# A two-part encoder layer on one core: attention, output projection and router input as one pipeline over token tiles

## The chip, the cores and the metric

One NeuronCore of a Trainium2 chip runs the whole layer as one program. It has five engines that work side by side, each on its own list of instructions, strictly in order: TensorE (PE, matmuls and transposes, results into eight PSUM banks of 128 x 512 f32), VectorE (DVE), ScalarE (ACT), GpSimd (POOL) and SyncE (SP, which only issues transfers). They are tied together by semaphores. The metric is the device time of one execution in microseconds (us), lower is better.

## The reference

```
h = rms_norm(x, g) * (1 + sc1) + sh1            # x: 512 tokens x 1024; sc, sh, g1, g2 = silu(c) @ w_ada + b_ada
proj = h @ w_in                                 # 1024 -> 1024 (gMLP u, v) + 672 (latents of attention)
gm_out = u * (tril(W_s) @ LN(v) + b)            # 512 channels
q, k, v = latents, normalised, @ w_q_up, w_kv_up   # 8 heads, 96 wide, v 64 wide; QK-norm and rotary
mla_out = softmax(q k^T, chunk-causal) v        # 512 channels; token tile t sees key tiles 0..t
mixed = concat(rms_norm(gm_out), rms_norm(mla_out))
x = x + g1 * (mixed @ w_out)                    # 1024 x 1024
h2 = rms_norm(x, g) * (1 + sc2) + sh2
scores = sigmoid(h2 @ w_router)                 # 64 experts, group-limited top 8
x = x + g2 * (shared_expert(h2) + sum over the 8 chosen experts of w_e * expert_e(h2))
```

Everything is f32. Where the kernel needs full precision at TensorE's faster rate it splits an operand into an upper part (rounded to the short format) and a lower part (the rest), and makes three matmuls of one: upper x upper, upper x lower, lower x upper (`three_passes`).

## The kernel before

The 512 tokens are T = 4 tiles of 128; D = 1024 is C = 8 chunks of 128. The program is written by hand for each engine, and the order of the work on an engine is the order in which its block is written; nothing is scheduled by a planner.

The stages, in time: (1) twelve 2 MB blocks of `w_ada` arrive; blocks 0 and 2 are multiplied on PE (L613), the ten others on DVE (`ada_block`, L1229 to L1234, eight multiply-adds each) and summed over partitions by one matmul with ones; after block 3 the first normalised input `h` can be formed. (2) The input projections with f32 weights (L633), the up-projections of q, k and v, QK-norm and rotary on DVE (L1303 to L1324), transposes of q and k. Meanwhile POOL makes the upper and lower parts of `w_out` (L509, L511), two chunks at a time. (3) Attention, 32 heads-of-tiles i = 0..31, tile t = i // 8 in the order 0, 1, 2, 3. For each: `scores` on PE (one f32 matmul of (t+1)*128 columns into one of NSB = 4 banks), `row_max` on DVE (a memset of the masked corner and a reduce), `exponential` on ACT, `prob_transposes` on PE, `prob_copy` on ACT, `weighted_values` on PE. PE runs three scores ahead. After the fourth head of the next tile DVE turns the finished tile into `mixed` (`outputs`, L1344 to L1349). (4) When all tiles are through, one root on ACT, one reciprocal on DVE, the scaling of `mixed`, 32 transposes of it in six banks (L744), its upper part on ACT (L1066) and its lower part on DVE (L1370), for all 512 tokens at once. (5) The output projection: 8 groups of 24 matmuls (L574 to L576), and behind each tile on DVE the residual and the second norm (`residual` L1382 to L1385, `norm2` L1389 to L1391, with a root on ACT between). (6) Transposes of `h2` (L768), router (L778), sigmoid, then the choice of experts on DVE (L1400 to L1434), while PE computes the shared expert (L787). (7) A list of the rows of each expert is made on DVE by 16 rounds of MAX8 (L1518 to L1523), and (8) the 64 experts run one after the other: 3 MB of weights each, split into upper parts on ACT (L1103, L1109) and lower parts on DVE (L1466), rows gathered and scattered by indirect transfers of POOL.

What the change touches is (1), the making of the parts of `w_out` in (2), and all of (3) to (6), with SP's list for the stores of `h2` and the loads behind them. The loop over the experts in (8) keeps its instructions.

Of the kernel before, what the change touches and what calls it, by code (L numbers as in the profile page):

```python
# [29 lines left out]
P = 128  # L30
# [16 lines left out]
def trunk_kernel(nc, a, out):  # L47
# [21 lines left out]
    ADA_PE = (0, 2)  # L69
    ADA_DVE = tuple(j for j in range(ADA) if j not in ADA_PE)  # L70
    ADA_FIRST = 4
    MAXX = 32
    NSMALL = 9
    scale = float(QD) ** -0.5
# [5 lines left out]
    with ExitStack() as ctx:  # L80
# [48 lines left out]
        NSB, NTB = 4, 2  # L129
# [8 lines left out]
        mixT_high = at("mixT_high", 80, [P, C, S], F32R)  # L138
        mixT_low = at("mixT_low", 159, [P, C, S], F32R)
        h2 = at("h2_sb", 143, [P, T, D])  # L140
        h2T = at("h2T", 112, [P, C, S])
# [7 lines left out]
        sco = at("sco", 151, [P, T, NE])  # L149
        bia = at("bia", 152, [P, T, NE])  # L150
        rep = at("rep", 153, [P, T, NE])
        m8 = at("m8", 154, [P, T * N_GROUPS, 8])
# [20 lines left out]
        w_d = [at(f"w_d{i}", 72 + 8 * i, [P, FC, D]) for i in range(2)]  # L173
        gu_high = [at(f"gu_high{half}", kb, [P, 2, HC, FF], F32R) for half, kb in enumerate((16, 88))]
        gu_low = [at(f"gu_low{half}", kb, [P, 2, HC, FF], F32R) for half, kb in enumerate((24, 102))]
        d_high = at("d_high", 112, [P, FC, D], F32R)
        d_low = at("d_low", 120, [P, FC, D], F32R)
# [24 lines left out]
        def small(name, shape, dt=F32):  # L202
# [13 lines left out]
        epsc = small("epsc", [P, 1])  # L216
        freq = small("freq", [P, RH])
# [53 lines left out]
        (s_mm, nmax_ok, exp_ok, pT_tr, pT_ok, av_mm, o_ok, mix_v, oss_ok, ostd_ok, orstd_ok, mix_ok, mixT_tr, out_mm,  # L271
         x1_ok, ss2_ok, std2_ok, h2_ok, st_h2, h2T_tr, h2T_ok, rt_mm, sco_ok, selm_ok, pos_mm, lmat_ok, list_mm,
         list_ok) = (sem(n) for n in (
            "s_mm", "nmax_ok", "exp_ok", "pT_tr", "pT_ok", "av_mm", "o_ok", "mix_v", "oss_ok", "ostd_ok", "orstd_ok", "mix_ok",
            "mixT_tr", "out_mm", "x1_ok", "ss2_ok", "std2_ok", "h2_ok", "st_h2", "h2T_tr", "h2T_ok", "rt_mm",
            "sco_ok", "selm_ok", "pos_mm", "lmat_ok", "list_mm", "list_ok"))
        flip_set, key_ok, key_tr, found_ok, found_tr, foundT_ok, flip_mm, src_ok, wts_ok, st_w, w_ok = (sem(n) for n in (
            "flip_set", "key_ok", "key_tr", "found_ok", "found_tr", "foundT_ok", "flip_mm", "src_ok", "wts_ok", "st_w", "w_ok"))
# [99 lines left out]
        def _(sp):  # L378
            sp.dma_start(cT[:], a["c"].rearrange("b (p c) -> p (b c)", c=C)).then_inc(ld["c"], 16)
            w_in_v = a["w_in"][0].rearrange("(p c) n -> p c n", c=C)  # L380
            for j in range(ADA):
                i, _ = ada_buffer(j)
                if j >= ADA_FIRST:
                    before = j - ADA_FIRST if j < ADA_FIRST + 2 else j - 2
                    if before in ADA_PE:
                        sp.wait_ge(ada_pe, ADA_PE.index(before) + 1)
                    else:
                        sp.wait_ge(ada_dve, ADA_DVE.index(before) + 1)
# [1247 lines left out]
```

## Time and profile before

| | us |
|---|---|
| three runs | 1123.85, 1121.76, 1113.04 |
| median | 1121.76 |
| the profiled execution, whole | 1113.93 |
| its span, first to last instruction | 1112.0 |
| PE, DVE, ACT, POOL busy in the span | 971.8, 905.2, 602.3, 278.4 |

The profile page gives busy time by engine, the span in 40 slices, the costliest groups of instructions, and the chain of waits that ended last. "PEclk" is the granted TensorE clock as a share of 2.4 GHz; it has two levels, 1.00 and 0.50. A busy PE is not a PE at its peak: a matmul's record runs to its modelled end and overlaps the next, so the pace is read from the starts. The whole time of an execution is 1.9 us more than its span here.

### The profile page before, as it was taken

The numbers are of one execution on the slowest core, as the hardware profiler recorded it, in microseconds if no ns is written. First come the engines' busy times: TensorE is split into PE (matmuls) and PEld (weight loads), VectorE is DVE, ScalarE is ACT, GpSimd is POOL, SyncE is SP. The second block draws the span as 40 slices with busy tenths as digits, with TensorE's granted clock in tenths as the row PEclk, the third lists the DMA queues.
The fourth block names the chain that finished last, engine by engine and source line by source line (L and its number), as shares of the span: only waits on it lengthen the run. The fifth ranks groups of instructions, "written<-read, shape, count | busy, mean of one in ns | idle before, by whom it ended". The sixth has DMA issues, their size and how long they took to land.

```text
span 1112.0 us, 14197 instructions
## 1 busy us (share of the span) xinstructions
PE 971.8 (87%) x4335; PEld 745.7 (67%) x4336; DVE 905.2 (81%) x1280; ACT 602.3 (54%) x948; POOL 278.4 (25%) x186
## 2 busy tenths in 40 slices
PE   3797899898999979898999988989897999898895
PEld 1354375586788657677777777777676777677684
DVE  3687877754566878998999999999998899898894
ACT  1123153466113046676777766667675767676672
POOL 1004105130000202323234232332323232324232
PEclk9899899889999989999999999999999999999897
DMA  9976402200027278999999999999999999999973
GB/s 310 393 280 232 151 1 76 104 2 1 19 89 276 67 294 268 374 318 339 325 340 359 344 333 339 326 337 333 327 349 327 309 333 356 351 327 350 341 257 59
DMA packets 86232, 286.79 MB, mean 258 GB/s; under 512 B 18052, under 2 KB 18564, under 8 KB 77112
## 3 DMA queue, kind: packets, MB, share of 16 engines
q1 hardware_dynamic: 64240, 248.03, 61.1%
q0 software_dynamic: 19056, 36.89, 13.2%
q10 hardware_dynamic: 2904, 1.48, 0.5%
q8 instruction: 16, 0.26, 0.1%
q14 instruction: 16, 0.13, 0.0%
HBM read 283.04 MB, written 37.88 MB: 289 GB/s over the span
## 4 chain that ended last, share of the span: by engine, by line
DMA 49%; PE 29%; DVE 11%; issue 6%; ACT 1%; SPq 1%; POOL 1%; POOLq 0%; DVEq 0%; ACTq 0%
DMA out<-oute,src_tab 44%; PE bank L633 5%; PE bank L574 4%; PE bank L575 4%; PE bank L576 4%; DMA xe<-h_rows,src_tab 3%; DMA ada_w<-in_w_ada 2%; DVE ada_acc L1234 2%; PE bank L787 2%; PE bank L708 2%; PE bank L725 1%; DVE gu_low L1466 1%; DVE q_sb L1313 1%; PE bank L804 1%; PE bank L716 1%
## 5 line engine op out<-in xcount | busy, mean ns | idle before, releaser
L1466 DVE TENSOR_TENSOR gu_low<-w_gu,gu_high 128x1024 fp32r<-128x1024 f32 x256 | 301.4, 1218 | 10.6 <-ACT gu_high L1103 5.4
L1103 ACT CAST gu_high<-w_gu 128x1024 fp32r<-128x1024 f32 x256 | 256.6, 1055 | 62.8 <-PE bank L576 57.2
L530 POOL DMA_INDIRECT out<-oute,src_tab x64 | 128.9, 2015 | 465.0 <-DMA out<-oute,src_tab 357.5
L574 PE MATMUL bank<-gu_high,xeT_high 128*128 128x512 f32 x512 | 208.1, 406 | 2.8 <-DVE xeT_low L1466 2.6
L576 PE MATMUL bank<-gu_high,xeT_low 128*128 128x512 f32 x512 | 202.1, 395 | 0.0
L575 PE MATMUL bank<-gu_low,xeT_high 128*128 128x512 f32 x512 | 201.8, 394 | 0.0
L1466 DVE TENSOR_TENSOR d_low<-w_d,d_high 128x1024 fp32r<-128x1024 f32 x128 | 150.4, 1216 | 0.0
L1109 ACT CAST d_high<-w_d 128x1024 fp32r<-128x1024 f32 x128 | 128.1, 1053 | 18.0 <-PE bank L576 18.0
L820 PE MATMUL bank<-ident,xe 128*128 128x128 f32 x512 | 73.5, 288 | 60.3 <-DMA xe<-h_rows,src_tab 58.4
L820 PEld LDWEIGHTS bank<-ident,xe 128*128 128x128 f32 x512 | 64.5, 194 | 81.3 <-issue 77.6
L574 PE MATMUL bank<-d_high,hwT_high 128*128 128x512 f32 x256 | 112.3, 439 | 6.7 <-DVE hwT_low L1466 6.5
L1466 DVE TENSOR_TENSOR xeT_low<-bank,xeT_high 128x512 fp32r<-128x512 f32 x128 | 82.2, 684 | 42.8 <-ACT xeT_high L1119 40.9
L574 PEld LDWEIGHTS bank<-gu_high,xeT_high 128*128 128x128 f32 x512 | 97.2, 190 | 23.1 <-DVE xeT_low L1466 2.7
L576 PEld LDWEIGHTS bank<-gu_high,xeT_low 128*128 128x128 f32 x512 | 96.7, 189 | 22.6
L575 PEld LDWEIGHTS bank<-gu_low,xeT_high 128*128 128x128 f32 x512 | 96.8, 189 | 19.9 <-issue 0.2
L524 POOL DMA_INDIRECT xe<-h_rows,src_tab x64 | 95.9, 1499 | 50.1 <-issue 45.7
L576 PE MATMUL bank<-d_high,hwT_low 128*128 128x512 f32 x256 | 106.7, 417 | 0.0
L575 PE MATMUL bank<-d_low,hwT_high 128*128 128x512 f32 x256 | 106.0, 414 | 0.0
L1119 ACT CAST xeT_high<-bank 128x512 fp32r<-128x512 f32 x128 | 68.9, 590 | 63.5 <-PE bank L820 63.5
L1502 DVE TENSOR_TENSOR oute<-bank,mod_rows 128x512 f32<-128x512 f32 x128 | 82.0, 682 | 10.8 <-PE bank L576 10.7
L1234 DVE SCALAR_TENSOR_TENSOR ada_acc<-ada_w,cact,ada_acc 128x512 f32<-128x512 f32 x70 | 64.2, 918 | 2.5
L574 PEld LDWEIGHTS bank<-d_high,hwT_high 128*128 128x128 f32 x256 | 52.5, 205 | 16.8 <-DVE d_low L1466 4.6
(278 smaller groups left out, 1291.6 us busy)
## 6 DMA issues: line engine op xcount, KB each, us to landing
w_gu<-in_w_exp_gate SPq DMA_DIRECT2D x128, 512.0 KB
w_gu<-in_w_exp_up SPq DMA_DIRECT2D x128, 512.0 KB
w_d<-in_w_exp_down SPq DMA_DIRECT2D x64, 1024.0 KB, 8.6
ada_w<-in_w_ada SPq DMA_DIRECT2D x12, 2048.0 KB, 11.9
w_out_sb<-in_w_out SPq DMA_DIRECT2D x2, 2048.0 KB, 7.2
w_lat_sb<-in_w_in SPq DMA_DIRECT2D x1, 2688.0 KB, 21.9
x_sb<-in_x SPq DMA_DIRECT2D x1, 2048.0 KB, 24.2
w_v_sb<-in_w_in SPq DMA_DIRECT2D x1, 2048.0 KB, 10.3
```

The costliest lines, as they stand in the source:

```text
L524: pool.indirect_dma_start(xe[i][:], None, h2_dram, bass.IndirectOffsetOnAxis(ap=rows, axis=0), bounds_check=last_row, oob_is_err=False).th ...
L530: pool.indirect_dma_start(out_rows, bass.IndirectOffsetOnAxis(ap=rows, axis=0), oute[i][:], None, bounds_check=last_row, oob_is_err=False, ...
L574: pe.matmul(dst, xh, wh, start=start, stop=False)
L575: pe.matmul(dst, xh, wl, start=False, stop=False)
L576: return pe.matmul(dst, xl, wh, start=False, stop=stop)
L820: last = pe.transpose(bank[c // 4][:, c % 4 * P:(c % 4 + 1) * P], xe[b][:, c:D:C], ident[:])
L1103: act.copy(gu_high[half][:, m], w_gu[half][i][:, m]).then_inc(gu_high_ok[half], 1)
L1109: act.copy(d_high[:, m], w_d[i][:, m]).then_inc(d_high_ok, 1)
L1119: act.copy(xeT_high[i][:, m * HC:(m + 1) * HC, :], bank[m][:].rearrange("p (c n) -> p c n", c=HC)).then_inc(xe_high_ok, 1)
L1234: ins = dve.scalar_tensor_tensor(acc[n % 2][:], w[:, c, :], cact[:, c:c + 1], acc[n % 2][:], ALU.mult, ALU.add)
L1466: return dve.tensor_tensor(low, whole, high.bitcast(F32), ALU.subtract)
L1502: last = dve.tensor_tensor(oute[i][:, cols], bank[4 + m][:], mod[:, GATE2, cols], ALU.mult)
```

## The change

The 32 heads are still 32, but the tiles go 3, 2, 1, 0 (`TILES`), the tile with most keys first; p is the place in that order. Scores use two banks instead of four (NSB = 2) and PE runs two scores ahead; one bank holds the weighted values, one (`T_BANK`) all transposes, two the output projection. While tile p is in attention, the finished tile p-1 goes through normalisation, transposes, split and output projection, and tile p-2 through residual, second norm, transposes and router. On each engine a function `between_heads(p, hd)` says what comes behind head hd of tile p. The roots of both norms no longer go to ACT: DVE computes them with a bit trick and three Newton steps (`rsqrt_mean`, 12 instructions on one or two columns). The gain `out_norm_g` moves from `mixed` into the weights: ACT forms the upper part of `w_out` times gain (8 x 128x1024), POOL scales the chunk and subtracts (8 + 8 instructions of 128x1024, where it had 4 + 4 of 128x2048). In (1) `x` is loaded first, each of blocks 0 to 3 is halved between PE and DVE, and the gain row is finished in two halves. PE's first half of the shared expert's first product stands ahead of the last router transposes; SP waits for the last score before it loads the shared weights and for the last output projection before it goes on to the experts' weights; the store of the last tile of `h2` moves to POOL.

```diff
-        NSB, NTB = 4, 2
+        NSB, NTB = 2, 2
+        O_BANK, T_BANK, Y_BANK = 4, 5, 6
+    TILES = tuple(reversed(range(T)))
+    W_ORDER = tuple(range(C // 2, C)) + tuple(range(C // 2))
 # SP
+            store_h2(0)
+            store_h2(1)
+            sp.wait_ge(s_mm, NI)
...
+            store_h2(2)
+            sp.wait_ge(out_mm, 2 * T)
 # POOL
+            for n in range(C):
+                c = W_ORDER[n]
                 pool.wait_ge(wout_high_ok, n + 1)
+                pool.tensor_scalar(w_out[:, c], w_out[:, c], on_g[:, c:c + 1], None, ALU.mult).then_inc(wout_scaled, 1)
+                pool.wait_ge(wout_scaled, n + 1)
+                pool.tensor_tensor(w_out_low[:, c], w_out[:, c], w_out_high[c // 2][:, c % 2].bitcast(F32), ALU.subtract).then_inc(wout_ok, 1)
 # PE
+            OUT_CUTS = (0, 3, 6, 9, 12, 2 * C)
+            def between_heads(p, hd):
+                if p >= 1:
+                    if hd in (1, 2):
+                        mixed_transposes(p - 1, hd - 1)
+                    if hd >= 3:
+                        out_projection(p - 1, OUT_CUTS[hd - 3], OUT_CUTS[hd - 2])
+                if p >= 2:
+                    if hd in (4, 5):
+                        h2_transposes(p - 2, hd - 4)
+                    if hd == 6:
+                        router(p - 2)
 # ACT
+            def between_heads(p, hd):
+                if p == 0 and hd < C // 2:
+                    wout_high(C // 2 + hd)
+                if p >= 1 and hd in (1, 2):
+                    mixed_high(p - 1, hd - 1)
+                if p >= 2:
+                    if hd in (4, 5):
+                        h2T_copy(p - 2, hd - 4)
+                    if hd == 6:
+                        logits(p - 2)
 # DVE
+            def rsqrt_mean(col, n):
+                k = col.shape[1]
+                y, sq, half = root[:, 0:k], root_sq[:, 0:k], root_half[:, 0:k]
+                link(dve.tensor_scalar(col, col, 1.0 / n, EPS, ALU.mult, ALU.add))
+                dve.tensor_scalar(half, col, -0.5, None, ALU.mult)
+                link(dve.tensor_scalar(y.bitcast(I32), col.bitcast(I32), -0.5, float(0x5F375A86), ALU.mult, ALU.add))
+                for step in range(3):
+                    link(dve.tensor_tensor(sq, y, y, ALU.mult))
+                    link(dve.tensor_tensor(sq, sq, half, ALU.mult))
+                    link(dve.scalar_tensor_tensor(y if step < 2 else col, sq, 1.5, y, ALU.add, ALU.mult))
+            def between_heads(p, hd):
+                if p >= 1:
+                    if hd == 0:
+                        outputs(p - 1)
+                    if hd in (1, 2):
+                        mixed_low(p - 1, hd - 1)
+                if p == 1 and hd == 3:
+                    second_gain()
+                if p >= 2:
+                    if hd == 2:
+                        residual(p - 2)
+                    if hd == 3:
+                        norm2(p - 2)
+                if hd == 6:
+                    link(square_sum(p, 0))
+            row_max(0)
+            for i in range(NI):
+                if i + 1 < NI:
+                    row_max(i + 1)
+                between_heads(*divmod(i, H))
```

DVE before, around the fourth head of a tile: a score's maximum is a MEMSET and a TENSOR_REDUCE, and `outputs` of the tile before stands between two of them once in eight heads.

```order
L1339 MEMSET bank 64x64 [waits s_mm]
L1340 TENSOR_REDUCE nmax<-bank 128x1 [waits dve_step]
L1344 RECIPROCAL den<-den 128x8 [waits av_mm]
L1345 TENSOR_TENSOR mixed<-bank,den 128x512 [waits dve_step]
L1349 ISA osq,oss<-mixed 128x512 [waits o_ok]
L1349 ISA oss 128x1
L1349 ISA osq,oss<-mixed 128x512
L1349 ISA oss 128x1
L1339 MEMSET bank 64x64 [waits s_mm,dve_step]
L1340 TENSOR_REDUCE nmax<-bank 128x1 [waits dve_step]
```

DVE now, behind `outputs` (which has grown by `rsqrt_mean` and two scalings), heads 0 to 3 of tile place p = 2.

```order
L1435 TENSOR_SCALAR mixed<-mixed,oss 128x512
L1406 MEMSET bank 64x64 [waits s_mm]
L1407 TENSOR_REDUCE nmax<-bank 128x1 [waits dve_step]
L1440 TENSOR_TENSOR mixT_low<-bank,mixT_high 128x512 [waits mixT_high_ok]
L1406 MEMSET bank 64x64 [waits s_mm]
L1407 TENSOR_REDUCE nmax<-bank 128x1 [waits dve_step]
L1440 TENSOR_TENSOR mixT_low<-bank,mixT_high 128x512 [waits mixT_high_ok]
L1449 TENSOR_TENSOR xtmp<-bank,mod_rows 128x512 [waits out_mm]
L1451 TENSOR_TENSOR x_sb<-x_sb,xtmp 128x512 [waits x1_ok]
L1449 TENSOR_TENSOR xtmp<-bank,mod_rows 128x512 [waits out_mm,dve_step]
L1451 TENSOR_TENSOR x_sb<-x_sb,xtmp 128x512 [waits x1_ok]
L1406 MEMSET bank 64x64 [waits s_mm,dve_step]
```

So the maximum of each of the next three scores now stands behind a step that itself waits for ACT, or behind four or more full-width operations.

PE now, heads 1 and 2 of the second tile in the order: the transposes of `mixed` stand between a head's weighted values and the next score.

```order
L707 MATMUL bank<-kT,qT 128x384 [waits exp_ok]
L715 MATMUL bank<-ident,prob_91 128x128 [waits pT_ok,exp_ok]
L715 MATMUL bank<-ident,prob_91 128x128 x2
L725 MATMUL bank<-vv_sb,probT_93 128x64 [waits pT_ok]
L725 MATMUL bank<-vv_sb,probT_93 128x64 x2
L738 MATMUL bank<-ident,mixed 128x128 [waits mix_ok]
L738 MATMUL bank<-ident,mixed 128x128 x3
L707 MATMUL bank<-kT,qT 128x384 [waits exp_ok]
L715 MATMUL bank<-ident,prob_92 128x128 [waits pT_ok,exp_ok]
L715 MATMUL bank<-ident,prob_92 128x128 x2
```

Before, nothing but scores, transposes and weighted values stood on PE between the first score and the last head.

## Rows read from the trace of the kernel before

**Rows 1.** Windows by stage: stretch, length, busy time of each engine, granted clock, DMA share, GB/s.
```profile
219.00:271.00 52.00, 51.14 (x304) 42.08 (x304) 25.63 (x82) 34.20 (x99) 12.37 (x4) 0.86 0.00 1
271.00:285.00 14.00, 6.17 (x35) 5.88 (x34) 10.15 (x20) 8.30 (x14) 0.00 (x0) 0.76 0.00 0
285.00:328.50 43.50, 43.50 (x193) 35.97 (x193) 21.93 (x30) 0.88 (x3) 0.00 (x0) 1.00 0.09 37
328.50:340.00 11.50, 11.17 (x99) 10.99 (x98) 5.29 (x7) 5.92 (x11) 0.00 (x0) 1.00 0.87 323
340.00:354.00 14.00, 14.00 (x69) 12.32 (x68) 9.92 (x61) 6.17 (x8) 2.05 (x4) 1.00 0.99 379
436.00:1112.00 676.00, 602.83 (x2794) 488.20 (x2792) 611.84 (x730) 462.41 (x664) 214.52 (x122) 0.97 0.95 323
```

**Rows 2.** Windows around the two falls of the granted clock.
```profile
214.00:232.00 18.00, 16.21 (x66) 14.28 (x67) 4.94 (x23) 13.09 (x40) 12.76 (x4) 0.50 0.01 2
271.00:275.00 4.00, 0.13 (x2) 0.00 (x0) 3.36 (x10) 1.53 (x4) 0.00 (x0) 0.90 0.00 0
275.00:281.00 6.00, 4.34 (x21) 4.35 (x22) 2.98 (x5) 4.29 (x7) 0.00 (x0) 0.50 0.00 0
```

**Rows 3.** Timeline of PE, tiles 2 and 3: start us, us, engine, line, operation, count.
```profile
245.87 0.86 PE L708 MATMUL bank<-kT,qT 96*128 96x384 f32 x2
247.51 0.86 PE L708 MATMUL bank<-kT,qT 96*128 96x384 f32 x2
...
260.88 1.08 PE L708 MATMUL bank<-kT,qT 96*128 96x512 f32 x2
...
263.07 0.65 PE L708 MATMUL bank<-kT,qT 96*128 96x512 f32 x1
```

**Rows 4.** Timeline of DVE and ACT for one head of tile 3.
```profile
262.19 0.69 DVE L1340 TENSOR_REDUCE nmax<-bank 128x1 f32<-128x512 f32 x1
...
262.92 0.69 ACT L1042 ACTIVATE prob<-bank,nmax 128x512 f32<-128x512 f32 x1
263.50 0.20 ACT L1042 ACTIVATION_READ_ACCUMULATOR prob<-bank,nmax 128x1 f32 x1
```

**Rows 5.** Timeline of DVE: the last `outputs`, and two small chained operations.
```profile
271.40 0.69 DVE L1345 TENSOR_TENSOR mixed<-bank,den 128x512 f32<-128x512 f32 x1
...
274.05 0.49 DVE L1365 TENSOR_SCALAR mixed<-mixed,oss 128x512 f32<-128x512 f32 x1
...
345.44 0.18 DVE L1414 TENSOR_SCALAR gmask<-grank 128x32 f32<-128x32 f32 x1
345.65 0.18 DVE L1415 TENSOR_SCALAR gneg<-gmask 128x32 f32<-128x32 f32 x1
```

**Rows 6.** Timeline of DVE: square sum and second norm of one tile.
```profile
297.53 1.22 DVE L1385 CUSTOM_DVE_ANT_0 h_sb<-x_sb 128x1024 f32<-128x1024 f32 x1
299.33 1.28 DVE L1390 SCALAR_TENSOR_TENSOR h_sb<-x_sb,ss,mod_rows 128x1024 f32<-128x1024 f32 x1
300.65 1.23 DVE L1391 TENSOR_TENSOR h_sb<-h_sb,mod_rows 128x1024 f32<-128x1024 f32 x1
```

**Rows 7.** Timeline, PE: the first router product and the transposes ahead of it.
```profile
328.46 1.04 PE L768 MATMUL bank<-ident,h_sb 128*128 128x128 f32 x8
...
330.79 1.90 PE L778 MATMUL bank<-w_r_sb,h2T 128*128 128x64 f32 x16
```

**Rows 8.** Timeline of DVE: block 3 of `w_ada`, and the first MAX8 of the expert lists.
```profile
38.70 5.47 DVE L1234 SCALAR_TENSOR_TENSOR ada_acc<-ada_w,cact,ada_acc 128x512 f32<-128x512 f32 x7
...
354.00 0.43 DVE L1518 MAX8 found<-bank 128x8 f32<-128x256 f32 x1 [3.23 <-PE bank L863]
```

**Rows 9.** Timeline of DVE and POOL while POOL splits weights.
```profile
106.66 1.50 POOL L491 CAST w_kv_high<-w_kv_sb 128x1024 fp32r<-128x1024 f32 x1
108.24 2.66 POOL L493 TENSOR_TENSOR w_kv_low<-w_kv_sb,w_kv_high 128x1024 fp32r<-128x1024 f32 x1
...
180.98 15.45 DVE L1313 TENSOR_TENSOR q_sb<-q_sb,qn_g 128x768 f32<-128x768 f32 x4
```

More of the change, by code:

```diff
@@ new lines, in h2_transposes @@
+            def h2_transposes(p, half):
+                if half == 0:
+                    pe.wait_ge(h2_ok, p + 1)
+                    pe.wait_ge(mixT_low_ok, 2 * min(p + 2, T))
+                    if p == T - 1:
+                        pe.wait_ge(logit_ok, p)
+                else:
+                    pe.wait_ge(h2T_ok, 2 * p + 1)
+                for c4 in range(4):
+                    last = pe.transpose(bank[T_BANK][:, c4 * P:(c4 + 1) * P], h2[:, TILES[p], half * 4 + c4::C], ident[:])
+                last.then_inc(h2T_tr, 1)
@@ new lines, in router @@
+            def router(p):
+                t = TILES[p]
+                pe.wait_ge(ld["wr"], 16)
+                pe.wait_ge(h2T_ok, 2 * p + 2)
+                for c in range(C):
+                    last = pe.matmul(bank[T_BANK][:, 0:NE], h2T[:, c, t * P:(t + 1) * P], w_r[:, c, :], start=(c == 0), stop=(c == C - 1))
+                last.then_inc(rt_mm, 1)
+            OUT_CUTS = (0, 3, 6, 9, 12, 2 * C)
[10 more added lines that the diff above has]
+                        router(p - 2)
@@ L729, in _ @@
+            for i in range(NSB):
                 scores(i)
@@ L788, in shared_gu, with shared_up @@
+            def shared_up(s):
+                t = TILES[s]
+                for c in range(C):
+                    last = pe.matmul(bank[4 + s % 2][:, FF:2 * FF], h2T[:, c, t * P:(t + 1) * P], ws_u[:, c, :], start=(c == 0), stop=(c == C - 1))
                 last.then_inc(sgu_mm, 1)
+            def shared_gu(s):
+                shared_gate(s)
+                shared_up(s)
             def shared_hT(t):
@@ L1377, in residual, with mixed_low @@
-            def residual(t):
+                    last = dve.tensor_scalar(mixed[:, t, s * GW:(s + 1) * GW], mixed[:, t, s * GW:(s + 1) * GW], oss[:, t, s:s + 1], None, ALU.mult)
+                last.then_inc(mix_ok, 1)
+            def mixed_low(p, half):
+                dve.wait_ge(mixT_high_ok, 2 * p + half + 1)
+                dve.tensor_tensor(mixT_low[:, half * 4:half * 4 + 4, :], bank[T_BANK][:].rearrange("p (c n) -> p c n", c=4),
+                                  mixT_high[:, half * 4:half * 4 + 4, :].bitcast(F32), ALU.subtract).then_inc(mixT_low_ok, 1)
@@ L1397, in _ @@
+            dve.wait_ge(gate_ok, GG)
+            row_max(0)
+            for i in range(NI):
+                if i + 1 < NI:
+                    row_max(i + 1)
+                between_heads(*divmod(i, H))
+            outputs(T - 1)
+            mixed_low(T - 1, 0)
+            mixed_low(T - 1, 1)
+            residual(T - 2)
+            norm2(T - 2)
+            residual(T - 1)
+            norm2(T - 1)
             dve.wait_ge(sco_ok, 1)
-            dve.wait_ge(st_h2, 16 * T)
+            dve.wait_ge(st_h2, 16 * (T - 1))
```

398 lines of the change are left out of this document (192 added, 206 removed).

## The prediction

> **What bounds the kernel now.** I read the windows by stage first, then the starts on PE inside the stages that the change rewrites, then DVE and ACT between two of those starts.
>
> The windows [rows 1] cut the span into a preparation, the loop over the experts from 436 us on, and the stages between. In the loop the transfers are busy 95% of 676 us and DVE 91% of it; the change leaves every instruction of it as it was, so I take the loop to start earlier or later and not to run faster. Attention, 219 to 271, has PE busy 51.1 of 52.0 us; the output projection, 285 to 328.5, has it busy the whole 43.5. Only 271 to 285 is poor: 6.2 of 14.0. So from the first score (219.15) to the last router product (340) PE has work for about 113 of 121 us. A pipeline over tiles can fill only what is idle there, some 8 us, and may save part of what a low clock costs: from 214 to 232 the granted clock stands at 0.50, the lower of its two levels [rows 2].
>
> The reader should see in [rows 3] the pace of a head: 263.07 - 260.88 = 2.19 us in tile 3, 247.51 - 245.87 = 1.64 us in tile 2, PE back to back. And in [rows 4] what a head needs outside PE: maximum 0.69 us and its memset (0.84 together), exponential 0.69 + 0.20 us.
>
> **The stage from first score to last router product, part by part.**
>
> *First tile (3), nothing beside it.* 8 heads x 2.19 = 17.5 us [rows 3]. The first score, its maximum and exponential come ahead, about 2.9 us (PE 1.08, then rows 4). The clock is low at the start, as before; 10 us at half rate cost 5 us. Together 25.4 us. The four casts of `w_out` that ACT gets between heads (1.05 us each) lie beside PE at half rate and cost nothing; at full rate ACT would need 0.9 + 0.5 + 1.05 = 2.5 us for a head of 2.19, 0.3 us each.
>
> *Three tiles with the pipeline: PE's work.* Attention of 52.0 us, less 6.7 for its low clock (13 us at half rate) and less tile 3's 17.5, leaves 27. Three output projections are 3/4 of 43.6 = 32.7. Transposes of `mixed` 3 x 1.05 and of `h2` 2 x 1.05, router 2 x 1.75 (1.04 per 8 transposes, 1.90 with its overlap per router, [rows 7]). Sum 68 us.
>
> *What PE waits for there.* PE is in order and has two scores ahead; the transposes of head i+2 need the maximum of i+2, which now stands behind `between_heads` of head i on DVE.
> Head 0: `outputs` costs a reciprocal 0.23, the product 0.73 and the square sum over as many columns as much again [rows 5], then 12 tiny operations. Two chained ones start 0.21 us apart (345.65 - 345.44), so about 2.3 us, and two scalings of 0.44 to 0.49: 5.0 us. Maximum and exponential of the next head follow: 6.7 us after the last weighted values. PE meanwhile has a head and a score, 2.4 us: it stands for 4.3 us in the second tile. In the third and fourth the last piece of projection (2.7 us) covers part; 2.1 and 2.7 remain.
> Heads 1 and 2: PE transposes, ACT copies (0.7 with its semaphore), DVE subtracts (0.75), and only then the next maximum and exponential (1.4): 2.9 us less the next score, 2.2 us of waiting, in each of six places. In the third and fourth tile the residual, four operations of 0.69 = 2.9 us, is added at head 2.
> Head 3, third and fourth tile: `norm2` is 1.22 + 2.3 + 1.32 + 1.23 = 6.1 us [rows 6], then maximum and exponential, against 2.05 us of projection and a score on PE: 3.8 and 4.0 us.
> Sum: 9.1 at head 0, 13 + 5.8 at heads 1 and 2, 7.8 at head 3: 35.7 us.
>
> *Tail.* After the last piece of the third projection: PE work for transposes 2 x 1.05 + 1.05, projection 10.9, routers 2 x 1.73, the first half of the shared gate and up 3.5: 21.0 us. It waits for `outputs` of the last tile (2.6 beyond the cover), for the split between its halves (1.4), for `norm2` of tile place 2, which DVE begins only after its residual (5.2), four ACT copies of 0.7, and the last residual and norm, 7.7 us against 3.5 of the shared gate (4.5). Together 16.7 idle, 37.7 in all.
>
> *Clock.* In [rows 2] the clock still stood at 1.00 when PE went idle at 271, was at 0.50 from 275, and needed until 281 to come back. In 214 to 232 it stayed low for 18 us over small matmuls, with PE counted as busy. I charge 2 us for each of three tile changes and 3 us for the tail: 9 us. The bounds are 0 and 20.
> The Trainium skill, page "TensorE: Matmul & The Clock Gate", section "HAM oscillation — how this bites in real kernels", says that bursts of matmuls with idle gaps between them let the clock fall and rise again and again, so that small holes cost more than their length. By it this term is not optional: without it the stage would be 9 us shorter. The two falls in this trace agree, and it speaks against a schedule with a hole of 2 to 5 us every few heads.
>
> Sum: 25.4 + 68 + 35.7 + 37.7 + 9 = 176 us, against 120.8 before: **+55 us**.
>
> **The other parts.** *Start.* Block 3 is multiplied by eight operations on DVE, the last seven in 5.47 us [rows 8]. Halved, DVE needs four (2.9 us) and PE's half runs beside it; the bias row goes ahead and the gain in two halves. 3.1 + 0.5 + 0.6 gives **-4.2 us**. Both orders put the same bytes (four blocks and x) in one queue before the last of block 3, so its arrival stays.
> *Parts of w_out.* POOL's subtraction of 128x1024 took 2.66 us and a cast 1.50 [rows 9]; the multiply by a per-row gain isn't in the trace, so it lies between 1.5 and 2.7, and I take 1.5, the row with one input like it. 8 x (1.5 + 2.66) = 33 us of POOL instead of 28. While POOL works on two inputs, DVE's operations of two SBUF inputs crawl: four of 0.95 us took 15.45 [rows 9]. The first half of the chain stands there again, 16.6 to 21 us of POOL instead of 15.1, but in eight pieces, and a DVE operation seems to get through per piece. Between -1 and +5; I take 0. The second half falls into the first tile, where DVE reads PSUM, and is done before the first projection.
> The Trainium skill, page "GPSIMD Engine Reference", section "1. Specifications", names contention of GpSimd with DVE instructions that have two SBUF inputs. By it the maxima, one PSUM input each, are untouched; the runs will have to show it, since in the profile before POOL is idle during tile 3.
> *Behind the router.* Before, DVE stood 3.23 us for the transposed keys [rows 8], behind 14 us of shared products on PE. 3.5 us of these now come first: **-3.4 us**. The weights of the first experts are asked for earlier too, but they were in before the row lists were ready (their stretch of full transfer is 340 to 354, [rows 1], and the lists start only then), so that gives nothing.
>
> Total: 55 - 4.2 + 0 - 3.4 = +47 us. Against the profiled execution, 1113.9, this is 1161. The median of the three runs stands 7.8 us above that execution, and they spread over 10.8; I add 3 and forecast **1164 us**. About 1% (11 us) is what a measurement of this kernel can tell from no change.
>
> **Rivals.**
> *The holes are filled (faster or the same).* If DVE and ACT ran their extra steps while PE worked off projection and scores, the 35.7 us and the 9 us would go: 47 - 45 = +2, 1116 to 1124; if in the tail norm2 were hidden too, -8, about 1108 to 1112. For it: DVE is busy 25.6 us of 52 in attention and 21.9 of 43.5 in the projection [rows 1], so by sums there is room. Against: every engine is in order, and a maximum behind a 5 us step is 5 us late. It decides for this rival if the step takes less than PE's two scores and a projection piece, about 2.4 us at head 0. Chance 0.14 (0.05 faster, 0.09 the same).
> *Half of it.* The small operations cost less than 0.21 us, neighbouring waits overlap, the clock holds: about +25, 1139 to 1145. Chance 0.22.
> *The clock stays low.* If short matmuls between waits hold it at 0.50 through the three tiles and the tail, as from 214 to 232, the dense projections too run at half rate for part of their time: 10 to 25 us more, 1175 to 1190. Chance 0.16.
> *POOL is late or slow.* A multiply of 2.66 or worse makes 43 us of POOL; the QK-norm loses up to 5 us, and the first projection could wait: +52, inside my range.
> The forecast with its neighbourhood (1150 to 1175) has 0.48.
>
> The range takes in the half case and the low clock: 1135 to 1188. Chances: faster 0.05, same 0.09, slower 0.86.
>
> **What would show it.** In the new profile: (1) the first `h` about 4 us earlier, near 45 us; (2) attention and projection as one stretch of some 115 to 140 us with PE idle for 50 of the 176, its waits named by ACT's exponential and by `mix_ok`; (3) row maxima on DVE that start straight after `outputs`, `mixed_low` or `norm2` although their score has long been there; (4) PEclk at 0.50 in several pieces of 230 to 380; (5) the first MAX8 of the lists near 400 us instead of 354, and the loop from there as long as before, 676 us. I am wrong if PE is busy over 90% from first score to router, or if the loop itself changes its length.

## The result, and the profile after

| | before | after |
|---|---|---|
| median of the runs, us | 1122.8 (1113.04 to 1124.77) | 1175.04 (1170.46 to 1178.06) |
| the profiled execution: span | 1112.0 | 1174.5 |

The change makes the kernel slower: ratio 1.048, 95% interval 1.041 to 1.055. The forecast was 1164 us (1135 to 1188). Ratios, here and below, are of means and leave out executions more than 1.5% above the fastest one of the same kernel, while medians are over all, so a ratio need not be the quotient of two medians. The profiled span grew by 62.5 us, more than the medians (52.2), since the profiled execution of before was one of its short ones. The page of the changed kernel, busy time by engine and the granted clock in 40 slices of 29.4 us:

```profile
PE 994.6 (85%) x4339; PEld 756.8 (64%) x4340; DVE 924.4 (79%) x1376; ACT 604.4 (51%) x951; POOL 296.4 (25%) x195
...
PEclk9897999968877798999999999999999999999998
```

PE is busy 23 us longer than the 971.8 of before; the slices from the ninth to the fourteenth show the low clock. The windows by stages of my own choice (first tile alone; three tiles with the pipeline; tail; router to the first MAX8 of the lists; loop), columns as in [rows 1]:

```profile
216.00:238.20 22.20, 21.12 (x128) 15.31 (x128) 10.37 (x25) 16.86 (x34) 16.56 (x7) 1.00 0.00 1
238.20:354.30 116.10, 83.34 (x395) 66.48 (x393) 52.12 (x159) 23.93 (x79) 4.16 (x2) 0.78 0.07 28
354.30:397.00 42.70, 30.02 (x121) 24.38 (x122) 19.76 (x51) 5.22 (x9) 0.80 (x1) 0.74 0.36 133
397.00:410.30 13.30, 13.30 (x55) 11.25 (x54) 9.94 (x62) 2.60 (x6) 1.88 (x4) 0.81 0.34 135
498.00:1174.00 676.00, 601.52 (x2779) 487.38 (x2777) 609.48 (x727) 461.75 (x660) 212.48 (x121) 0.97 0.95 322
```

From first score to last router product it is 22.2 + 116.1 + 42.7 = 181.0 us where [rows 1] had 120.8. In the middle stage PE is busy 83.3 of 116.1 us. The last row answers to the last of [rows 1]: 676 us of the loop with the same busy times within 0.5% (POOL's within 1%).

What PE waited for, from 237 to 343 us (first row) and from 345 to 400 (the others): us in total, times, the longest.

```profile
PE bank L715 <- ACT prob L1094: 31.2, 15, 6.8
```
```profile
PE bank L765 <- DVE h_sb L1458: 4.2, 1, 4.2
PE bank L738 <- DVE mixed L1435: 2.2, 1, 2.2
PE bank L583 <- DVE xtmp L1449: 2.1, 1, 2.1
PE bank L773 <- ACT h2T L1113: 1.5, 2, 0.8
PE bank L738 <- DVE mixT_low L1440: 1.4, 1, 1.4
PE bank L765 <- ACT h2T L1113: 1.4, 2, 0.7
```

The first row names the exponential, but that only passes on what DVE did. The timeline of the changed kernel around the first tile change shows it:

```profile
236.97 0.69 DVE L1429 TENSOR_TENSOR mixed<-bank,den 128x512 f32<-128x512 f32 x1
...
237.70 1.12 DVE L1423 CUSTOM_DVE_ANT_0 osq<-mixed 128x512 f32<-128x512 f32 x1
...
239.07 0.97 DVE L1414 TENSOR_SCALAR root_half<-oss 128x2 f32<-128x2 f32 x1
...
240.27 2.19 DVE L1418 TENSOR_TENSOR root_sq<-root_sq,root_half 128x2 f32<-128x2 f32 x1
...
243.86 0.88 DVE L1435 TENSOR_SCALAR mixed<-mixed,oss 128x512 f32<-128x512 f32 x2
244.75 0.11 DVE L1406 MEMSET bank<- 64x64 f32 x1
244.89 0.56 DVE L1407 TENSOR_REDUCE nmax<-bank 128x1 f32<-128x384 f32 x1
245.48 0.58 ACT L1094 ACTIVATE prob<-bank,nmax 128x384 f32<-128x384 f32 x1 [8.10 <-DVE nmax L1407]
...
246.21 0.90 PE L715 MATMUL bank<-ident,prob 128*128 128x128 f32 x3 [6.84 <-ACT prob L1094]
```

The score of head 10 was written at 239.4 (its matmuls start at 238.50). Its maximum starts only at 244.75, in the same 0.01 us in which the scaling of `outputs` ends. ACT had been idle for 8.1 us, PE for 6.8.

Of the 8 us of `outputs` three are GpSimd's: a square sum of 1.12 instead of 0.69, two one-input operations on two columns of 0.97 and 0.90, one two-input operation of 2.19 instead of 0.16. The slowed operations end when an instruction of GpSimd ends: the first two at 240.04 us against its 240.00, the last at 242.46 against its 242.44. GpSimd's instructions (the first is an earlier one, beside DVE's two-input operations):

```profile
192.21 4.33 POOL L515 TENSOR_SCALAR w_out_sb<-w_out_sb,on_g 128x1024 f32<-128x1024 f32 x1
...
237.16 2.84 POOL L515 TENSOR_SCALAR w_out_sb<-w_out_sb,on_g 128x1024 f32<-128x1024 f32 x1
240.09 2.35 POOL L517 TENSOR_TENSOR w_out_low<-w_out_sb,w_out_high 128x1024 fp32r<-128x1024 f32 x1
```

### The profile page after: what moved, and what is told of

The parts are those of the page before. It is cut to its first block, busy times and chain, and to the rows that moved or that the text cites. A ratio compares the mean times of both kernels' runs of the same rounds, so it can differ in the third digit from the quotient of the medians.

```text
span 1174.5 us, 14351 instructions
## 1 busy us (share of the span) xinstructions
PE 994.6 (85%) x4339; PEld 756.8 (64%) x4340; DVE 924.4 (79%) x1376; ACT 604.4 (51%) x951; POOL 296.4 (25%) x195
## 4 chain that ended last, share of the span: by engine, by line
DMA 47%; PE 30%; DVE 13%; issue 6%; ACT 2%; POOL 1%; POOLq 0%; SPq 0%; DVEq 0%; ACTq 0%
DMA out<-oute,src_tab 43%; PE bank L631 5%; PE bank L583 4%; PE bank L584 4%; PE bank L585 4%; DMA xe<-h_rows,src_tab 3%; PE bank L843 2%; PE bank L725 2%; DMA ada_w<-in_w_ada 1%; DVE ada_acc L1297 1%; PE bank L822 1%; PE bank L605 1%; PE bank L715 1%; DVE gu_low L1565 1%; PE bank L817 1%
## 5 line engine op out<-in xcount | busy, mean ns | idle before, releaser
L539 POOL DMA_INDIRECT out<-oute,src_tab x64 | 133.2, 2081 | 468.9 <-DMA out<-oute,src_tab 353.3
L533 POOL DMA_INDIRECT xe<-h_rows,src_tab x64 | 88.9, 1389 | 51.0 <-DVE src_tab L1637 25.6
## 6 DMA issues: line engine op xcount, KB each, us to landing
w_v_sb<-in_w_in SPq DMA_DIRECT2D x1, 2048.0 KB, 12.8
```

What stands on the lines that cost most here:

```text
L533: pool.indirect_dma_start(xe[i][:], None, h2_dram, bass.IndirectOffsetOnAxis(ap=rows, axis=0), bounds_check=last_row, oob_is_err=False).th ...
L539: pool.indirect_dma_start(out_rows, bass.IndirectOffsetOnAxis(ap=rows, axis=0), oute[i][:], None, bounds_check=last_row, oob_is_err=False, ...
```

## The theories

A (that of the prediction): PE waits because the next row maximum stands behind a long step on DVE's in-order list; the low clock is a consequence. B: the low clock is the larger cost. D: the chain score, maximum, exponential, transposes with only two score banks limits a head, whatever stands between. The recorded expectations give letters to their own rivals, so B and C in e1's are other cases than here; each is to be read with its condition. All runs in one table; "stage" is from the start of the first score matmul to the start of the last router matmul in the profiled execution, and ratios are to runs of the kernel before on the same chip (its medians were 1122.8, 1120.7, 1120.7 and 1121.4; e1 to e4, e5 to e8 and e9 to e11 each shared theirs).

| run | median us | ratio, 95% | stage | first h |
|---|---|---|---|---|
| before | 1121 to 1123 | | 120.4 | 49.1 |
| changed | 1175.0 | 1.048 (1.041 to 1.055) | 180.6 | 45.4 |
| changed, again | 1173.1 | 1.051 (1.042 to 1.060) | 180.8 | 46.7 |
| e1 idle time filled | 1171.6 | 1.045 (1.040 to 1.050) | 175.9 | 46.0 |
| e2 finer, one head apart | 1135.3 | 1.012 (1.007 to 1.018) | 142.3 | 46.3 |
| e3 tiles 0, 1, 2, 3 | 1179.2 | 1.052 (1.047 to 1.058) | 187.9 | 46.2 |
| e6 less GpSimd | 1172.5 | 1.052 (1.044 to 1.059) | 177.3 | 45.9 |
| e7 one Newton step | 1161.2 | 1.043 (1.034 to 1.051) | 169.5 | 46.1 |
| e8 shared product first | 1168.7 | 1.050 (1.041 to 1.059) | 178.4 | 45.7 |
| e4 before, blocks and x of the start | 1141.1 | none | 146.2 | 51.4 |
| e5 before, whole start | 1117.5 | 1.000 (0.997 to 1.004) | 130.0 | 45.5 |
| e9 before, tiles 3 to 0 | 1112.5 | 0.996 (0.992 to 1.000) | 121.3 | 49.4 |
| e10 both | 1110.5 | 0.994 (0.990 to 0.999) | 118.3 | 46.0 |

For steps of a few us the intervals are too wide; there I go by the stage in the profile. The changed kernel's stage came out at 180.6 and 180.8 in two executions:

> The changed kernel unchanged, for a time beside the same executions of the kernel before: 1.048, as when it was first timed; this tells whether ratios of different groups of executions can be compared within 0.5%.

It came out at 1.051, 0.003 off: within 0.5%, no closer.

## Experiments on the pipeline

**e2: the same instructions, cut and shifted.** On DVE, p the place of the tile:

```diff
                     if hd == 0:
                         outputs(p - 1)
-                    if hd in (1, 2):
-                        mixed_low(p - 1, hd - 1)
+                    if hd == 1:
+                        outputs_scaled(p - 1)
+                if p >= 2 and hd in (3, 4):
+                    residual(p - 2, (hd - 3,))
+                if p >= 2 and hd == 5:
+                    norm2_sum(p - 2)
+                if p >= 1 and hd in (3, 5):
+                    mixed_low(p - 1, (hd - 3) // 2)
...
+                if p >= 2 and hd == 6:
+                    norm2_root(p - 2)
+                if p >= 2 and hd == 7:
+                    norm2_scaled(p - 2)
```

On PE the transposes of `mixed` stand behind heads 2 and 4, ScalarE's copies of them behind 3 and 5, the first half of a projection behind heads 4 to 7, its second half behind heads 0 to 2 of the next tile; the transposes of `h2` and the router come one tile later, and `shared_up(0)` ahead of the last of them.

> The changed kernel with the same work cut finer and placed with a distance of a head between engines: outputs and norm2 in two and three pieces of at most 3.3 us behind different heads, ScalarE's and VectorE's split of mixed one head behind TensorE's transposes, the second half of each output projection under the first three heads of the next tile, the first shared product whole ahead of the last transposes of h2. The same instructions in another order. Theory A (order on VectorE makes the holes): of 31 us of waits between 237 and 343 us about 20 go, of the low clock 10 to 20 us, of the tail some 5: 30 to 45 us faster than the changed kernel, 1.00 to 1.02 of the kernel before. Rival D (the latency of the chain score, maximum, exponential, transposes with two score banks limits a head, whatever stands between): less than 12 us faster. Rival B: 15 to 22 us faster, clock as low as now.

```profile
238.50:310.00 71.50, 62.97 (x346) 52.46 (x345) 50.80 (x153) 22.82 (x76) 5.12 (x2) 0.93 0.03 10
...
310.00:359.80 49.80, 42.75 (x192) 35.79 (x191) 20.92 (x58) 6.82 (x13) 0.81 (x1) 0.82 0.42 154
```
```profile
PE bank L715 <- ACT prob L1103: 8.3, 5, 4.3
```

These are e2's windows (pipeline, tail) and its wait for the exponential from 238 to 310 us. The waits fell from 31.2 us in 15 places to 8.3 in 5, the clock over the three tiles rose from 0.78 to 0.93, the stage is 38.3 us shorter. DVE does the same 50.8 us of work. Theory A holds, by its own numbers; D falls, since the two score banks and the handshakes are the same. What e2 shows is the worth of order on all three engines, since it moves pieces of PE and ACT too; the part of DVE's lengths is shown by e7. Still 1.2% slower than before: PE's work did not shrink, and the tail alone is 50 us.

**e1: idle time filled.** 158 matmuls whose results nobody reads (the expectation counts one less), ahead of PE's waits, 38 of them in the tail:

```diff
+            FILL = {9: 28, 10: 6, 11: 6, 17: 7, 18: 7, 19: 18, 25: 9, 26: 9, 27: 19, 28: 4, 29: 3, 30: 4}
+            def fill(b, n):
+                for _ in range(n):
+                    pe.matmul(bank[b][:, 0:P], ident[:], ones[:], start=True, stop=True)
...
+                    fill(NSB + (i + 1) % NTB, FILL.get(i, 0))
                     prob_transposes(i + 1)
```

> The changed kernel, with idle TensorE time filled: 157 short matmuls (128x128, ident times ones) into a transpose or score bank that is free at that point, placed where TensorE waited longest (28 before the 7 us wait, 18 and 19 before the two waits of 4.6 and 4.8 us, 5 to 9 before those of 1.5 to 2.3 us, 16 in the tail). Their results are never read. Theory A (holes by in-order waits, and the low clock as their consequence): the waits themselves stay, but the clock holds at 1.00 over most of 237 to 397 us, where 51 us of TensorE's busy time ran at 0.50; half of that comes back where TensorE sets the pace: 12 to 25 us faster than the changed kernel, near 1.03 of the kernel before. Rival B (the low clock costs little because VectorE and the handshakes set the pace): within 5 us of the changed kernel. Rival C (the fills themselves come too late or too long): slower than the changed kernel.

Windows of e1: first tile, then 237 to 343, then the rest; and its wait from 237 to 343.

```profile
217.00:237.00 20.00, 19.00 (x115) 13.72 (x115) 8.68 (x22) 15.81 (x31) 14.36 (x6) 1.00 0.00 1
237.00:343.00 106.00, 93.08 (x615) 80.92 (x615) 51.40 (x152) 24.55 (x80) 6.37 (x3) 1.00 0.08 31
343.00:393.00 50.00, 42.89 (x231) 37.17 (x229) 22.16 (x60) 5.59 (x11) 0.80 (x1) 0.86 0.28 103
```
```profile
PE bank L715 <- ACT prob L1105: 12.4, 13, 3.0
```

The clock now stands at 1.00 through all 106 us, so it was the holes that let it fall. But the stage is only 4.7 us shorter: expected were 12 to 25, and what came is the rival of "within 5 us". Behind each of the 16 groups of fills PE still waited, 0.10 to 2.50 us, so the fills were never what held it up. At full clock PE comes earlier to the same waits, whose end DVE sets. In the changed kernel 47 us of PE's busy time ran at half rate (30.7 in the three tiles, 16.5 in the tail; the 51 of the expectation are the time that the clock was low in the three tiles). e1 brought back 34 of the 47, 17 us on paper, for 4.7 us: most of it lay in time that would have been waiting otherwise. The Trainium skill, page "TensorE: Matmul & The Clock Gate", section "HAM oscillation — how this bites in real kernels", has small holes cost more than their length: the clock followed it, the time did not, because the holes were another engine's.

**e7: fewer operations on DVE.** `for step in range(3)` becomes `range(1)` in `rsqrt_mean`; the roots lose precision.

> The changed kernel with one Newton step instead of three in each root (the roots are exact to about 0.2% only). Six operations of 0.20 us less in each of eight roots. Theory A (every us of a step on VectorE is a us of waiting on TensorE, since the next maximum stands behind it): of five roots in the loop and three in the tail all but the one of the last outputs come back in full and more where the clock is low: 8 to 12 us faster than the changed kernel. Rival (VectorE's length does not set the pace, the handshakes do): under 3 us.

The stage is 11.1 us shorter, as expected of A. PE waits for seven of the eight roots (not for `norm2` of tile place 2, which is hidden behind the last projection); six operations of 0.20 us less in each are 8.2 us. The other 3 may be the clock's (between the first tile and the last router matmul it was low for 51 us here, for 73 in the changed kernel), but no run shows that. A length on DVE is paid in full on PE here.

**e6: no multiplication on GpSimd in the first tile.**

```diff
+                if n < C // 2:
                     pool.tensor_scalar(w_out[:, c], w_out[:, c], on_g[:, c:c + 1], None, ALU.mult).then_inc(wout_scaled, 1)
```

> The changed kernel without GpSimd's four multiplications of the second half of w_out (these four chunks' lower parts lack the gain). Theory: GpSimd is through with w_out at 231 instead of 242.4 us, before outputs of the first tile, which then takes 5.0 us as I had worked out (0.69 each for the square sum, 0.2 for each small operation) instead of 8.0; the longest wait of TensorE (6.8 us) falls to about 4, and the whole is 3 us faster. Rival: outputs stays at 7 to 8 us, since its length comes from its own chain and not from GpSimd.

Its timeline of DVE at the first tile change, and PE's wait behind it:

```profile
237.28 0.20 DVE L1429 RECIPROCAL den<-den 128x8 f32<-128x8 f32 x1 [0.42 <-PE bank L726]
...
241.21 0.88 DVE L1436 TENSOR_SCALAR mixed<-mixed,oss 128x512 f32<-128x512 f32 x2
242.10 0.11 DVE L1407 MEMSET bank<- 64x64 f32 x1
```
```profile
243.56 0.90 PE L716 MATMUL bank<-ident,prob 128*128 128x128 f32 x3 [3.66 <-ACT prob L1095]
```

`outputs` takes 4.8 us and PE waits 3.66 instead of 6.84; the stage is 3.3 us shorter. The length was GpSimd's.

**e8: `shared_up(0)` ahead of the last transposes too.**

> The changed kernel with the second half of the first shared product (3.5 us at full clock) ahead of the last transposes of h2 too. TensorE waits 4.2 us there for norm2 of the last tile. Theory: the wait falls to about 0.7, the router ends when it did, and the shared products behind it are through 3.5 us earlier: 2 to 4 us faster. Rival: the lists for the experts, which hang on the router alone, set what follows: no change.

```profile
390.06 0.71 PE L765 MATMUL bank<-ident,h_sb 128*128 128x128 f32 x4 [0.70 <-DVE h_sb L1458]
```

The wait for the last `h2` fell from 4.2 to 0.70 us. From first score to first scatter it is 264.8 us (216.3 to 481.0) instead of 268.1 (216.0 to 484.1): 3.4 us, the size that was expected, but not by the expected way. The router does not end when it did: the last router matmul comes 2.2 us sooner (stage 178.4), because the clock, which fell at 388.4 us in the wait of the changed kernel, stands at 1.00 here until 395.6. From there to the first MAX8 it gains 2.1 us, and loses 1.0 of it up to the first scatter. The whole time cannot show it: 1.050 with an interval of 0.018.

**e3: tiles in the order 0, 1, 2, 3.** `TILES = tuple(range(T))`.

> The changed kernel with its tiles in the order 0, 1, 2, 3 instead of 3, 2, 1, 0, and one wait more for the last store of h2 (it reads the memory that the row keys go to). Theory A: TensorE's own work is the same 68 us, but the longest heads (2.19 us against 0.55) now stand beside the pipeline's steps, so a step of 5 us on VectorE is covered by more of it: waits of 31 us fall to about 20, and the first tile without a pipeline takes 8 us instead of 20, with the second half of the parts of w_out late by up to 10 us behind it. Sum: 5 to 15 us faster than the changed kernel. Rival (longest first is right, parts of w_out and the longer tail decide): 5 us or more slower.

Windows of e3 to 255 us, PE's longest wait, and DVE's last step before it:

```profile
217.00:255.00 38.00, 23.59 (x88) 18.48 (x89) 20.19 (x51) 15.77 (x48) 20.73 (x8) 0.52 0.00 1
```
```profile
238.73 3.26 DVE L1435 TENSOR_SCALAR mixed<-mixed,oss 128x512 f32<-128x512 f32 x2
```
```profile
243.22 0.69 PE L715 MATMUL bank<-ident,prob 128*128 128x128 f32 x2 [9.22 <-ACT prob L1094]
```

A miss: the stage is 7.3 us longer, not 5 to 15 shorter, and the rival is what came. The first tile is short now, so its `outputs` lie wholly under GpSimd's work on `w_out` (230.9 to 242.0 us, 11 instead of 4.8), and the clock stands at 0.50 from 219 to 255, which neither side had named. The tail, the rival's other reason, is hardly longer: 45.8 us from the last weighted values to the last router matmul against 45.1 in the changed kernel. By the stage longest first is the better order here (the ratios, 1.052 against 1.048 and 1.051, do not tell them apart); how the 7.3 us divide between GpSimd and the clock was not taken apart.

## Experiments on the start and the order of the tiles

**e4: the start alone, on the kernel before.** `x` first, blocks 0 to 3 halved, the gain row in two halves.

> The kernel before with only the change of the start: x first, blocks 0 to 3 halved between TensorE and VectorE, the gain row finished in two halves. My sum: the first h 4.2 us earlier (measured in the changed kernel: 45.4 instead of 49.1) and the whole about 4 us faster, 0.996. Rival: the first h is earlier but the gain is lost on the way to attention (later blocks of w_ada come when they came before): within 1 us.

The first `h` in e4's timeline of DVE, and the window of its attention:

```profile
51.41 1.29 DVE L1250 SCALAR_TENSOR_TENSOR h_sb<-x_sb,ss,mod_rows 128x1024 f32<-128x1024 f32 x1
```
```profile
221.00:291.00 70.00, 69.16 (x243) 54.01 (x244) 24.04 (x78) 28.46 (x88) 11.56 (x4) 0.51 0.00 1
```

Both forecasts failed: the first `h` came at 51.4, later than the 49.1 of before. PE's part of each block waits for a copy on DVE (`cbc`) of the silu of `c`, and here that copy starts at 19.8 us. In the changed kernel it starts at 4.96:

```profile
4.96 0.69 DVE L1269 COPY cbc<-cact 128x1024 f32<-128x1024 f32 x1 [4.85 <-ACT cact L986]
```

The change also moves ScalarE's nine small loads behind the silu of `c`, two lines of the diff that my sum passed over. The second row is 70 of the 78 us of e4's attention, with PE busy and the clock at 0.51. Its total is no measure: one execution took 1115.5 us and three took 1141 to 1143, and the profile is of one of the three.

**e5: with those two lines.**

```diff
             act.activation(cact[:], cT[:], ACT.Silu).then_inc(silu_c, 1)
+            for dst, src in smalls:
+                act.dma_start(dst, src, allow_slow_non_contiguous=True).then_inc(ld["small"], 16)
```

> The kernel before with the change of the start as in e4_start, and with ScalarE's nine small loads issued behind the silu of c instead of ahead of it. In the kernel before the silu starts at 17.9 us, behind 16 us of issues on ScalarE's own list; in the changed kernel at 4.7 us, and VectorE's copy of it (which TensorE's part of each block waits for) at 5.0 instead of 18.2. Theory: this move, which my sum left out, carries the start; e4_start without it had its first h at 51.4 us, later than before (49.1). With it the first h comes at 45.4 to 46.5 us, and the whole is 3 to 4 us faster than the kernel before, 0.997. Rival: the halved blocks are what carries it, and e4_start was late for another reason: the first h again near 51. Open: e4_start's clock stood at 0.50 through all of attention, 69 us, in most of its executions; if this depends on when the work of the start falls, it may be gone here.

The first `h` comes at 45.54 us, 3.5 earlier than before: without the early silu the halved blocks gain nothing, with it they gain this. The silu alone, with whole blocks, was not run, so how much the halving adds is open. The whole is unchanged, 1.000 (0.997 to 1.004). In its profile the first score is 3.3 us early (215.9) and the stage 9.6 us longer. The clock is low for 31 us of it, with PE busy throughout; before, it was low from 214 to 232 [rows 2].

```profile
217.70:248.40 30.70, 30.70 (x112) 25.43 (x113) 10.78 (x41) 14.40 (x53) 9.85 (x3) 0.50 0.00 1
```

**e9 and e10: tile 3 first, on the kernel before, without any pipeline.** `t = TILES[i // H]` in scores, maxima, exponentials, weighted values and `outputs`; e10 adds e5.

> The kernel before with one thing of the change: attention takes the tiles in the order 3, 2, 1, 0 (no pipeline, four score banks, everything else as before). In the kernels with tile 0 first the granted clock stood at 0.50 from the first scores on for 18 us (before), 33 us (e5_start_silu), 36 us (e3_natural) and 69 us (e4_start); in all with tile 3 first it stood at 1.00 there. Theory: the order decides this; with tile 3 first attention runs at full clock, 45 us instead of 52 as profiled and instead of up to 78: 7 us faster than the profiled execution of the kernel before, up to 10 in the median, and with less spread: 0.990 to 0.994. Rival (the clock is settled by what comes ahead of attention, or falls by chance): the clock low at 218 here too, within 2 us of the kernel before.

> The kernel before with both: the start of e5_start_silu and the tile order of e9_reversed. Theory: the start's 3.6 us come through once the clock doesn't eat them, and the order's 7 to 10 us: 10 to 14 us faster than the kernel before, 0.988 to 0.991, faster than both kernels. Rival: as e9_reversed, the start gain alone or nothing.

The first windows of attention in e9, then e10 up to 262 us and to its end:

```profile
219.00:223.00 4.00, 3.65 (x5) 1.58 (x6) 0.80 (x2) 2.13 (x3) 3.92 (x2) 0.50 0.00 0
223.00:267.00 44.00, 41.33 (x286) 34.15 (x284) 24.16 (x78) 27.79 (x87) 8.65 (x3) 1.00 0.01 1
```
```profile
216.00:262.00 46.00, 43.25 (x288) 34.82 (x288) 24.78 (x78) 29.58 (x87) 11.70 (x4) 1.00 0.01 1
262.20:266.00 3.80, 3.80 (x16) 3.45 (x16) 0.70 (x3) 2.79 (x12) 0.00 (x0) 0.50 0.00 0
```

The clock is back 3.8 us behind e9's first score, and in e10 it does not fall before 262.2 us. So the order decides the clock at the start of attention, as expected. The time is another matter: the gain is about half of what I expected, 0.4% and 0.6%, the first with an interval that touches 1. By the medians of all executions (1112.5 and 1110.5 against 1121.4) it would be 0.8% and 1.0%, as forecast; the kernel before spreads over 28 us and e9 over 12, so the size is uncertain.

In e9's profile attention takes 51.1 us from first score to last weighted values (219.4 to 270.5) against 52.0, and the stage up to the router 121.3 against 120.4. So the low clock has in part only moved: it falls at 267.6, among the short heads that now come last, and is low for 17 us up to the router, where before it was low for 7. Against e5, whose clock stayed low for 31 us, e10's attention gains 10.1 us (50.0 against 60.1). e10 is the fastest kernel of this study: 0.994 of before (0.990 to 0.999), 63 us faster than the changed one.

## Why the prediction was right, and where it was not

The sign, the size and the mechanism were right; the forecast of 1164 is 11 us below the median of 1175. That the stage came out within 5 us (176 against 181) is in part luck: first tile and waits were put 11.6 us too high, work and clock together 16.8 us too low. The steps, in us of the profiled executions:

| step | predicted | measured |
|---|---|---|
| first score earlier (start, parts of w_out) | -4.2 + 0 | -3.2 |
| first tile | 25.4 (5 of it clock) | 22.2, clock 1.00 |
| waits in three tiles | 35.7 | 31.2 |
| waits in the tail | 16.7 | 12.8 |
| work of PE in both | 68 + 21.0 | 116.1 + 42.7 - 44.0 = 114.8 |
| low clock beyond the first tile | 9 | in that: 23.6 |
| stage | 176 | 181.0 |
| router to first scatter | -3.4 | +2.2 |
| loop | 0 | +3.1 |
| sum of changes | +47 | +62.5 (with rounding) |

*Waits.* At the tile changes they were 6.8, 1.7 and 2.3 us (4.3, 2.1, 2.7 predicted), at heads 1 and 2 together 16.2 (18.8), but behind `norm2` only 0.2 and 1.1 (3.8 and 4.0): PE worked off the projection there at half rate and so was busy for as long as DVE. (The sum for attention's work has a slip: 52.0 - 6.7 - 17.5 is 27.8 and not 27.) The rest, 2.8 us, are waits of under 1 us that I had not listed. The lengths on DVE were right where GpSimd was idle: `outputs` (5.0 predicted) took 4.8 us at the third tile change and `norm2` (6.1) 6.0, as the changed kernel's DVE shows:

```profile
315.25 0.20 DVE L1428 RECIPROCAL den<-den 128x8 f32<-128x8 f32 x1 [0.83 <-PE bank L725]
...
320.07 0.11 DVE L1406 MEMSET bank<- 64x64 f32 x1
...
330.71 1.21 DVE L1455 CUSTOM_DVE_ANT_0 h_sb<-x_sb 128x1024 f32<-128x1024 f32 x1
...
335.47 1.22 DVE L1458 TENSOR_TENSOR h_sb<-h_sb,mod_rows 128x1024 f32<-128x1024 f32 x1
```

Only the first `outputs` was longer, 8 us; e6 shows why. I had POOL done "before the first projection" and read the end at 242.4 as harmless, though `outputs` has SBUF operands and lies before that.

*Clock.* This is the term that was mis-sized, 9 us for 23.6 of lost rate (half of the 47 us that PE was busy at the low clock). As a cost it was nearer than it looks: e1 took away 17 of the 23.6 and won 4.7 us, since waits and half rate share the same time. My sum added them as if they stood one behind the other. What I charged to the first tile (5 us) did not happen at all; e9 and e10 put that down to the order of the tiles.

*Start.* -3.6 us for the first `h` (4.2 predicted), but it needs a cause that I had not seen, ScalarE's list (e4, e5). Nor did the arrival of block 3 stay: DVE starts on it as it lands, at 36.90 us instead of 38.18, so 1.3 of the 3.6 us come from the loads. In the second profile of the changed kernel it was 2.3, and the first score came 1.3 us earlier and not 3.2: the start scatters by as much as it gains. *Parts of w_out.* The multiplication took 2.84 us with DVE on PSUM or idle and 3.6 to 4.3 beside DVE's two-input operations, outside my bounds of 1.5 to 2.7: I had bounded it by a cast, at the 1.50 of [rows 9], and a gain per partition costs more than a second input. On the path it cost little ahead of attention (3.2 of the 3.6 us of the start arrive at the first score in the first profile) and 3 us at the first tile change. The Trainium skill, page "GPSIMD Engine Reference", section "1. Specifications", names contention with DVE instructions that have two SBUF inputs or run in a 2-port mode. The maxima were untouched, as I read from it: all 32 took between 0.29 and 0.69 us by their width, beside GpSimd or not. The two slowed operations on SBUF with one input (0.97 and 0.90 us) are not of the two-input kind; whether they ran in a 2-port mode no run here shows.

*Behind the router.* The step failed. DVE's wait for the keys fell (3.23 to 2.03 us), but the first MAX8 comes 13.3 us after the router instead of 14.2, so 0.9 us earlier and not 3.4. The other 2.5 are the clock's, which was low up to 402.0 us, while PE worked on the shared products:

```profile
397.00:402.00 5.00, 5.00 (x13) 3.96 (x13) 4.10 (x37) 0.63 (x2) 0.00 (x0) 0.50 0.82 338
```

From there to the first scatter it takes 73.8 us instead of 70.7. The profiles of all kernels with the pipeline have 73.5 to 74.9 there, those without it 68.8 to 71.8, so this belongs to the change; its cause is open. *Loop.* 690.4 us from the first scatter to the end of the span against 687.3. The same kernel had 684.6 in its second profile and the others 682.5 to 688.4, with the same instructions, so this is scatter between executions.

*Rivals.* "The holes are filled" falls with 44 us of waits. "Half of it" falls. "The clock stays low" gave 1175 to 1190 and the median lies at its edge; the clock was indeed low for 73 of the 159 us of the three tiles and the tail, but e1 denies the price: at full clock the kernel is hardly faster. "POOL is late or slow" happened in part, 3 us at the first tile change (e6).

## What to carry to other kernels

Before you interleave stages, add up what the busiest engine has idle: here 8 to 9 us, and what the low clock takes; no pipeline could gain more in this stage, while each of its steps could cost. On an in-order engine what counts is not the sum of its work but the longest piece between two things that the bottleneck waits for: the same instructions cut to at most 3.3 us and put one head apart gave back 38 of 60 us. And when two engines' lists decide a start, read both: without the two moved lines on ScalarE the rewritten blocks, which had been credited with the gain, made the start later.

## What the runs showed of the hardware

- The granted clock in attention depended on the order of its tiles. With tile 0 first (heads of 128 columns) it stood at 0.50 for 14 us behind the first score (before), 31 (e5), 37 (e3) and 68 (e4, in an execution of 1141 us; another one took 1115.5), with PE busy 30.7 of 30.7 us in e5. With tile 3 first (512 columns) it was at 1.00 from the first score or within 3.9 us, in all nine profiles that have it so. The mean clock of whole executions agrees: 0.952 in e9 (12 executions) and 0.954 in e10 (12) against 0.946 before (23). So a busy PE alone does not bring the clock back; what it is in the order that does was not taken apart.
- A multiplication by a gain per partition of 128x1024 f32 on GpSimd took 2.84 us, more than a subtraction of two such tensors (2.35), which a count of its inputs would not have given.
- An operation of DVE on two columns took 2.19 us beside GpSimd, and 0.16 without it; it ended 0.02 us behind GpSimd's 2.35 us instruction, so here a tiny operation cost what was left of a long one.
